# Other query tiles for the side projections of attention, the last gate projection in the last head, and two copies ahead of the token factor

## The chip, the core and the metric

The kernel runs on one core of a Trainium2 chip. A core has TensorE (matrix products into PSUM), VectorE, ScalarE (activations by table), GpSimd, and SyncE, whose queue issues the transfers here. The metric is the device time of one execution in microseconds; lower is better.

## The reference

Two blocks of a network for 1024 tokens of width 1024, in float32:

```
x = x + short_conv_fourier_mixer(rms_norm(x), ...)     # layer 0
x = x + gqa_axial_mixer(rms_norm(x), ...)              # layer 1
x = rms_norm(x)
# second block: pooling and a bidirectional mLSTM, output projection, norm
```

The change lies in layers 0 and 1. Layer 1 is attention with 8 query heads of 128 and 2 key heads:

```
q, k, v, z = split(h @ w_in)
q = rope(rms_norm(q, q_gain));  k = rope(rms_norm(k, k_gain))
p = softmax(q k^T * 128**-0.5)
return ((p v) * silu(z)) @ w_out
```

## The kernel before, in words

Activations lie transposed: channels on partitions, the 1024 tokens along the row. A matrix product with a weight is cut into units of 128 output channels. To keep float32 accuracy, each operand is split into a high and a low part of the type fp32r, and three products are summed (high by high, high by low, low by high). GpSimd splits each weight unit: a cast makes `w_hi` (L600), a subtraction `w_lo` (L602). It has two slots, so unit u can be split when unit u-2 is done; the transfer of the next units runs in three slots of `w_raw`. A unit is 8 blocks of the contraction by 3 products by 2 halves of the tokens, 48 products of 512 columns into one of two PSUM banks, `pair[0]` and `pair[1]`; the engine that reads a bank out signals `pair_free`.

**Layer 0.** The factor of the RMS norm depends on the token alone, so the products run on data that are not normalised, and the factor `rstd_a` is multiplied in afterwards. TensorE makes units 0 and 1 interleaved while the input arrives, then sums the squares (`norm_stats`, L665). ScalarE makes the factor by logarithm and exponential (`norm_rstd`, L1071 and L1072; `ln_ahead`, L1069, is a logarithm of one column that loads the table early) and copies units 0 and 1 out of the banks (`bu`, L1101, and `ax_sb`, L1107). Unit 2 uses the bank of unit 0.

**Layer 1.** For each head h two units are needed: the query projection and the projection of its gate z. They are made during the attention of the head before, by `piece(h, which, c, part)`: `which` is 0 for the query and 1 for z, c is the half of the tokens, and part is one half of the contraction, 12 products at L782. All of them use one half bank, the "side bank", which VectorE or ScalarE must have read out (`bg_free`) before the next use. A head has 8 query tiles of 128 queries, t = 8h + i. For a tile, TensorE makes the scores (L810) two tiles ahead; VectorE takes the maxima (L1631); ScalarE makes the exponentials (L1191); VectorE divides by the sum (L1637, L1638); TensorE transposes the probabilities (`turn`, L823); ScalarE copies the high part (`turned`, L1199) and VectorE subtracts to get the low part (`turned_low`, L1402); and for every pair of tiles TensorE multiplies with the values (`weigh_values`, L835) and VectorE gates the result (L1656).

The next head's query goes a way of its own between these steps: the token factor (`q_token_half`, VectorE, L1605), its square and the swap of its halves (`raw`, ScalarE, L1136 to L1138), the rotation (`q_rotate_half`, VectorE, L1559 and L1562), the sum of its squares (`q_stats`, TensorE, L794), a copy of the sums (`q_sums`, ScalarE, L1172), logarithm and power (`head_ln`, `head_rstd`, L1146 and L1143), scaling (L1567), high and low part (L1150, L1402). The gate takes the token factor (`z_token_half`, L1617) and a Silu (L1185), for which ScalarE loads another table. Every engine works its instructions off in the order in which the code issues them; the order beside the tiles is written out by hand, on TensorE in the table `BESIDE`, on the others by conditions on i. In the last head, ScalarE and VectorE also prepare the operand of the output projection (`y_hi`, L1086, and `low`), from the gated values that went through DRAM.

Of the kernel before, what the change touches and what calls it, by code (L numbers as in the profile page):

```python
# [20 lines left out]
S = 1024  # L21
# [65 lines left out]
def build(nc, x_t, weight_units, channel_params, ident_in, dft_d, dft_s, rope, edge, masks, block_mask,  # L87
          qkv_blocks, gate_w, gate_b, pool_w, reset_mask, out):
    ctx = ExitStack()
    with ctx:  # L90
# [544 lines left out]
        def _(pe):  # L635
# [205 lines left out]
            for c in range(2):  # L841
# [11 lines left out]
            BESIDE = {0: [(0, 0, 0)], 1: [(0, 0, 1)], 2: [(0, 1, 0)], 3: [(0, 1, 1)],  # L853
                      5: [(1, 0, 0), (1, 0, 1)], 6: [(1, 1, 0)], 7: [(1, 1, 1)]}
            for t in range(QT * HEADS):
                h, i = t // QT, t % QT
                turn(t)
                if h + 1 < HEADS and i == 4:
                    q_stats(h + 1, 0)
                if t + 2 < QT * HEADS:  # L860
                    scores(t + 2)
                if h + 1 < HEADS:
                    if i == 4:
                        q_stats(h + 1, 1)
# [183 lines left out]
        def _(act):  # L1048
# [17 lines left out]

            def norm_rstd(count, sums, rstd, bias=eps_col):

                link(act.activation(ln_ahead[:, :], bias[:, :], ACT.Ln, bias=bias[:, :]))  # L1069
# [25 lines left out]
            norm_rstd(1, aux[:, 0:S], rstd_a)  # L1095
            for j in range(AB):
# [11 lines left out]
                signal(pair_free[(u + 1) % 2])  # L1108
                act.wait_ge(fft1_done, j + 1)
# [11 lines left out]
            for e in range(KT):  # L1121
                act.wait_ge(x_done, e + 1)
                gained(e, xa, "norm_odd", opb_hi)
                square(1, e, xa, sq_a, acc_a)
            norm_rstd(2, aux[:, 0:S], rstd_a)


# [3 lines left out]
            def raw(n, c, cols):  # L1131


                act.wait_ge(q_scaled, c + 1)
                half = P // 2
                link(act.activation(sq_b[:, cols], q_raw[:, 0, cols], ACT.Square), qsq)  # L1136
# [16 lines left out]
            for g in range(KV_HEADS):  # L1153
                raw(g, g, whole)
# [11 lines left out]
            def q_raw_half(h, c):  # L1166
                raw(KV_HEADS + h, KV_HEADS + 2 * h + c, columns(c))

            def q_sums(h, c):
# [4 lines left out]
                if c == 1:  # L1174
                    head_ln(rstd_b[:, :], whole)
                    head_rstd()
# [26 lines left out]
            for c in range(2):  # L1203
                q_raw_half(0, c)
# [24 lines left out]
            norm_squares(2, xc, sq_c, acc_c, KT)  # L1229


            norm_rstd(3, aux[:, S:2 * S], rstd_g, eps2_col)
            act.wait_ge(unit_done, BASE[4])
            split_norm(0, op_hi)

            norm_rstd(4, aux[:, 0:S], rstd_c)
# [155 lines left out]
            norm_squares(3, xf, sq_f, acc_f, 2 * KT)  # L1392
            norm_rstd(5, aux[:, 0:S], rstd_f)
# [3 lines left out]
        def _(dve):  # L1397
# [274 lines left out]
            for t in range(QT * HEADS):  # L1672
                h, i = t // QT, t % QT
                beside = h + 1 < HEADS
                if beside and i == 5:
                    scale_head(KV_HEADS + h + 1)
                turned_low(t)
# [14 lines left out]
                if not beside and i >= 1:  # L1692
                    low(i - 1, q_raw[:, (i - 1) % 2, :], OP0["y2"], opb_hi, opb_lo)
            gate_values(4 * HEADS - 1)

            low(KT - 1, y_b[:, (KT - 1) % 2, :], OP0["y2"], opb_hi, opb_lo)
# [397 lines left out]
```

## Time and profile before

| | |
|---|---|
| median of 3 runs | 1993.68 us (1992.86 to 2003.64) |
| the profiled execution | 1993.3 us, its span 1991.5 us |
| TensorE busy | 1819.2 us, 91% |
| VectorE busy | 1047.7 us, 53% |
| ScalarE busy | 582.2 us, 29% |
| GpSimd busy | 427.4 us, 21% |
| mean granted clock of TensorE | 0.968 |

The span is the time from the first to the last instruction of the profiled execution. Busy shares are sums over the whole program; where an engine stands, and for whom, is read from the rows of a stretch. In the timeline a row gives the start, the duration, the engine, the line and operation, the output and inputs, the count of instructions merged into it, and in brackets the idle time of the engine before it with the instruction that ended it. Durations of neighbouring matrix products overlap, so the time that one costs is the difference of two starts. Attention's tiles run from 504.54 to 964.70 us.

### The profile page before, as it was taken

How to read it: one execution, taken by the hardware profiler on the slowest of the kernel's cores; microseconds unless marked ns; L12 is line 12 of the kernel's file. 1: busy time of each engine (PE TensorE's matmuls, PEld its weight loads, DVE VectorE, ACT ScalarE, POOL GpSimd, SP SyncE). 2: the span in 40 equal slices, each digit the busy share in tenths (PEclk: the TensorE clock that was granted, in tenths of full speed). 3: DMA queues.
4: the chain of work that ended last, by engine and by line, in shares of the span. 5: the costliest groups of instructions: out<-in, count | busy, mean ns of one | idle time of the engine just before them, and what ended most of it. 6: DMA issues, size and time to landing. Idle time of an engine off the chain costs nothing. (4 is left out here: it accounts for less than half of the span.)

```text
span 1991.5 us, 21292 instructions
## 1 busy us (share of the span) xinstructions
PE 1819.2 (91%) x8440; PEld 1457.3 (73%) x8440; DVE 1047.7 (53%) x1441; ACT 582.2 (29%) x709; POOL 427.4 (21%) x234
## 2 busy tenths in 40 slices
PE   6999998999899999997896999999998888659996
PEld 5888887877778777776784766777886676447884
DVE  5243244344667676766535653233433788987113
ACT  5010012134555655655103211100225334132001
POOL 3233232232111011010122323333323000003230
PEclk9999999999999999999898999999999999879998
DMA  5011131141000000102420201121231001225102
GB/s 190 32 64 64 43 127 34 52 148 43 12 32 33 32 22 11 33 32 67 172 85 32 74 32 32 69 69 65 91 123 53 22 6 59 85 102 195 53 32 85
DMA packets 36915, 129.75 MB, mean 65 GB/s; under 512 B 4964, under 2 KB 5476, under 8 KB 36560
## 3 DMA queue, kind: packets, MB, share of 16 engines
q1 hardware_dynamic: 36816, 128.39, 18.2%
q8 instruction: 67, 1.10, 0.2%
q14 instruction: 32, 0.26, 0.0%
HBM read 96.68 MB, written 31.56 MB: 64 GB/s over the span
## 5 line engine op out<-in xcount | busy, mean ns | idle before, releaser
L600 POOL CAST w_hi<-w_raw 128x1024 fp32r<-128x1024 f32 x107 | 115.3, 1078 | 1324.9 <-issue 1309.4
L655 PE MATMUL pair<-op_hi,w_hi 128*128 128x512 f32 x1024 | 326.3, 400 | 34.2 <-DVE op_lo L1423 11.7
L655 PE MATMUL pair<-op_lo,w_hi 128*128 128x512 f32 x1024 | 319.1, 393 | 0.0
L655 PE MATMUL pair<-op_hi,w_lo 128*128 128x512 f32 x1024 | 318.6, 392 | 0.0
L602 POOL TENSOR_TENSOR w_lo<-w_raw,w_hi 128x1024 fp32r<-128x1024 f32 x107 | 279.7, 2614 | 8.6
L655 PEld LDWEIGHTS pair<-op_hi,w_hi 128*128 128x128 f32 x1024 | 193.3, 191 | 87.8 <-issue 38.7
L655 PEld LDWEIGHTS pair<-op_lo,w_hi 128*128 128x128 f32 x1024 | 194.8, 190 | 41.3
L655 PEld LDWEIGHTS pair<-op_hi,w_lo 128*128 128x128 f32 x1024 | 194.3, 190 | 41.3
L1402 DVE TENSOR_TENSOR pt_lo<-pair,pt_hi 128x1024 fp32r<-128x1024 f32 x64 | 78.3, 1224 | 106.7 <-ACT pt_hi L1199 106.1
L1199 ACT ACTIVATE pt_hi<-pair 128x1024 fp32r<-128x1024 f32 x64 | 65.7, 1027 | 147.6 <-PE pair L823 91.9
L782 PE MATMUL pair<-opb_hi,w_hi 128*128 128x512 f32 x256 | 100.3, 392 | 0.0
L782 PE MATMUL pair<-opb_hi,w_lo 128*128 128x512 f32 x256 | 99.8, 390 | 0.0
L782 PE MATMUL pair<-opb_lo,w_hi 128*128 128x512 f32 x256 | 99.6, 389 | 0.0
L823 PE MATMUL pair<-ident,prob 128*128 128x128 f32 x512 | 70.1, 282 | 26.6 <-DVE prob L1638 26.6
L823 PEld LDWEIGHTS pair<-ident,prob 128*128 128x128 f32 x512 | 59.2, 144 | 39.2 <-DVE prob L1638 37.3
L655 PE MATMUL pair<-o_hi,w_hi 128*128 128x512 f32 x256 | 80.6, 396 | 6.3 <-DVE o_lo L1402 5.6
L835 PE MATMUL pair<-pt_hi,v_hi 128*128 128x256 f32 x256 | 76.0, 297 | 8.2 <-DVE pt_lo L1402 8.2
L655 PE MATMUL pair<-o_lo,w_hi 128*128 128x512 f32 x256 | 79.8, 393 | 0.0
L655 PE MATMUL pair<-o_hi,w_lo 128*128 128x512 f32 x256 | 79.7, 393 | 0.0
L1631 DVE TENSOR_REDUCE stat_b<-aux 128x1 f32<-128x1024 f32 x64 | 78.4, 1225 | 2.4 <-PE aux L810 0.2
L1014 PE MATMUL aux<-v_tok,k_w 128*128 128x257 f32 x224 | 61.0, 396 | 16.1 <-DVE state L1863 12.9
L835 PE MATMUL pair<-pt_lo,v_hi 128*128 128x256 f32 x256 | 74.9, 292 | 0.0
(294 smaller groups left out, 3072.6 us busy)
## 6 DMA issues: line engine op xcount, KB each, us to landing
w_raw<-weight_units SPq DMA_DIRECT2D x107, 512.0 KB, 3.4
xf<-y_dram SPq DMA_DIRECT2D x14, 512.0 KB, 5.3
xa<-x_t SPq DMA_DIRECT2D x8, 512.0 KB, 8.4
x_dram<-xa SPq DMA_DIRECT2D x8, 512.0 KB, 6.4
xc<-x_dram SPq DMA_DIRECT2D x8, 512.0 KB, 8.2
x_dram<-xc SPq DMA_DIRECT2D x8, 512.0 KB, 2.6
y_dram<-y_d SPq DMA_DIRECT2D x8, 512.0 KB, 2.9
mz_dram<-y_d SPq DMA_DIRECT2D x8, 512.0 KB, 2.9
```

Of the source, the lines that this page charges most:

```text
L600: pool.tensor_copy(w_hi[:, u % 2, :], w_raw[:, u % 3, :]).then_inc(w_hi_done, 1)
L602: pool.tensor_tensor(w_lo[:, u % 2, :], w_raw[:, u % 3, :], w_hi[:, u % 2, :], ALU.subtract).then_inc(w_split, 1)
L655: mm = pe.matmul(acc[:, cols], w, x[:, kt0 + k, cols], start=(first and k == 0 and n == 0), stop=(last and k == KT - 1 and n == 2))
L782: mm = pe.matmul(bank, w, x[:, k, cols], start=(k == 0 and n == 0), stop=(k == KT - 1 and n == 2))
L823: mm = pe.transpose(pair[0][:, k * P:(k + 1) * P], prob[:, t % 2, k * P:(k + 1) * P], ident[:, :])
L835: mm = pe.matmul(pair[1][:, HALF:HALF + 2 * P], v[:, g, k, :], p[:, k, :], start=(k == 0 and n == 0), stop=(k == QT - 1 and n == 2))
L1014: mm = pe.matmul(o, k_w[:, d, i * P:(i + 1) * P], v_tok[:, h % 2, c, :], start=True, stop=True)
L1199: link(act.activation(pt_hi[:, :, (t % 2) * P:(t % 2 + 1) * P], pair[0][:, :].rearrange("p (k q) -> p k q", k=QT), ACT.Copy), pt_hi_ready)
L1402: link(dve.tensor_tensor(lo, full, hi, ALU.subtract), done)
L1631: link(dve.reduce_max(stat_b[:, t % 2, 2:3], aux[:, (t % 2) * S:(t % 2 + 1) * S], AX.X))
```

## The change

In layer 0 the table load for the logarithm is split off (`norm_ahead`), and in the first round ScalarE copies units 0 and 1 out before it makes the factor. The other norms keep the order that they had.

In attention, on TensorE: both parts of a query half stand in tiles 0 and 2, one each before in tiles 0 to 3; the first sum of squares moves from tile 4 to behind the scores of tile 3, the second from behind the scores of tile 4 to ahead of its transposition; the gate's four parts stand one each in tiles 4 to 7, before two in tile 5 and one each in 6 and 7. The gate projection of the last head moves from the head before into tiles 0 and 1 of the last head itself. On VectorE the token factors of the projections move ahead of the tile's subtraction, and the scaling of the head behind it. On ScalarE the square of the second half moves ahead of the copy of tile 3, the swap stays behind. The operand copies of the last head move one tile later.

```diff
-            BESIDE = {0: [(0, 0, 0)], 1: [(0, 0, 1)], 2: [(0, 1, 0)], 3: [(0, 1, 1)],
-                      5: [(1, 0, 0), (1, 0, 1)], 6: [(1, 1, 0)], 7: [(1, 1, 1)]}
+            def beside(t):
+                h, i = t // QT, t % QT
+                if h == HEADS - 1:
+                    for part in range(2):
+                        if i < 2:
+                            piece(h, 1, i, part)
+                    return
+                if i in (0, 2):
+                    for part in range(2):
+                        piece(h + 1, 0, i // 2, part)
+                if i == 3:
+                    q_stats(h + 1, 0)
+                if i >= 4 and h + 1 < HEADS - 1:
+                    piece(h + 1, 1, (i - 4) // 2, i % 2)
+
             for t in range(QT * HEADS):
                 h, i = t // QT, t % QT
+                if i == 4 and h + 1 < HEADS:
+                    q_stats(h + 1, 1)
                 turn(t)
-                if h + 1 < HEADS and i == 4:
-                    q_stats(h + 1, 0)
                 if t + 2 < QT * HEADS:
                     scores(t + 2)
-                if h + 1 < HEADS:
-                    if i == 4:
-                        q_stats(h + 1, 1)
-                    for which, c, part in BESIDE.get(i, []):
-                        piece(h + 1, which, c, part)
+                beside(t)
                 if i % 2:
                     weigh_values(t // 2)
...
-            norm_rstd(1, aux[:, 0:S], rstd_a)
+            norm_ahead()
             for j in range(AB):
...
                 signal(pair_free[(u + 1) % 2])
+                if j == 0:
+                    norm_rstd(1, aux[:, 0:S], rstd_a)
...
                 beside = h + 1 < HEADS
+                if beside and i == 3:
+                    q_square_half(h + 1, 1)
+                if beside and i == 4:
+                    q_sums(h + 1, 1)
                 turned(t)
-                if beside and i == 4:
-                    q_sums(h + 1, 0)
                 if t + 1 < QT * HEADS:
                     exponentials(t + 1)
-                if i == 1:
+                if i == (1 if beside else 2):
                     gate_silu(h)
+                if beside and i == 1:
+                    q_square_half(h + 1, 0)
+                    q_swap_half(h + 1, 0)
+                if beside and i == 3:
+                    q_sums(h + 1, 0)
+                    q_swap_half(h + 1, 1)
                 if beside and i == 4:
-                    q_sums(h + 1, 1)
+                    head_ln(rstd_b[:, :], whole)
+                    head_rstd()
                 if beside and i == 5:
                     q_hi_head(h + 1)
-                if beside and i in (1, 3):
-                    q_raw_half(h + 1, i // 2)
-                if not beside and i >= 1:
-                    y_hi("y2", i - 1, q_raw[:, (i - 1) % 2, :], opb_hi)
+                if not beside and i >= 2:
+                    y_hi("y2", i - 2, q_raw[:, (i - 2) % 2, :], opb_hi)
...
                 beside = h + 1 < HEADS
+                if beside and i in (1, 3):
+                    q_token_half(h + 1, i // 2)
+                if beside and h + 1 < HEADS - 1 and i == 6:
+                    z_token_half(h + 1, 0)
+                if beside and h >= 1 and i == 0:
+                    z_token_half(h, 1)
+                if not beside and i in (1, 2):
+                    z_token_half(h, i - 1)
+                turned_low(t)
                 if beside and i == 5:
                     scale_head(KV_HEADS + h + 1)
-                turned_low(t)
...
-                if beside and i in (1, 3):
-                    q_token_half(h + 1, i // 2)
-                if beside and i in (5, 7):
-                    z_token_half(h + 1, i // 2 - 2)
```

The order on ScalarE at the start of layer 0, before (`bu` and `ax_sb` are the copies of units 0 and 1):

```order
L1069 ACTIVATE ln_ahead<-eps_col 128x1
L1071 ACTIVATE rstd_a<-aux,eps_col 128x1024
L1072 ACT_TABLE_LOAD
L1072 ACTIVATE rstd_a<-rstd_a 128x1024
L1101 ACTIVATE bu<-pair 128x1024
L1107 ACTIVATE ax_sb<-pair 128x1024
```

and now:

```order
L1079 ACTIVATE ln_ahead<-eps_col 128x1
L1114 ACTIVATE bu<-pair 128x1024
L1120 ACTIVATE ax_sb<-pair 128x1024
L1084 ACTIVATE rstd_a<-aux,eps_col 128x1024
L1085 ACT_TABLE_LOAD
L1085 ACTIVATE rstd_a<-rstd_a 128x1024
```

Both copies stand ahead of the factor. The order on VectorE from the gating of tile 2 through tile 3 of a head (`q_raw<-pair,rstd_a` is the token factor of the next query's second half, the two rows of rotation before it belong to the first half), before:

```order
L1656 TENSOR_TENSOR y_b<-pair,sz_q 128x256
L1559 SCALAR_TENSOR_TENSOR q_raw<-q_raw,par,rope_sb 128x512 x2
L1562 TENSOR_TENSOR q_raw<-q_raw 128x512
L1402 TENSOR_TENSOR pt_lo<-pair,pt_hi 128x8x128
L1637 RECIPROCAL stat_b<-stat_b 128x1
L1638 TENSOR_SCALAR prob<-prob,stat_b 128x1024
L1631 TENSOR_REDUCE stat_b<-aux 128x1
L1632 TENSOR_SCALAR stat_b<-stat_b 128x1
L1605 TENSOR_TENSOR q_raw<-pair,rstd_a 128x512
```

and now:

```order
L1689 TENSOR_TENSOR y_b<-pair,sz_q 128x256
L1592 SCALAR_TENSOR_TENSOR q_raw<-q_raw,par,rope_sb 128x512 x2
L1595 TENSOR_TENSOR q_raw<-q_raw 128x512
L1638 TENSOR_TENSOR q_raw<-pair,rstd_a 128x512
L1435 TENSOR_TENSOR pt_lo<-pair,pt_hi 128x8x128
L1670 RECIPROCAL stat_b<-stat_b 128x1
L1671 TENSOR_SCALAR prob<-prob,stat_b 128x1024
L1664 TENSOR_REDUCE stat_b<-aux 128x1
L1665 TENSOR_SCALAR stat_b<-stat_b 128x1
```

The token factor moved from the end of tile 3 to ahead of its subtraction, directly behind the rotation. The order on ScalarE from tile 3 on (`sq_b<-q_raw` is the square, `sq_b<-pair` the copy of the sums, `q_raw<-q_raw` the swap), before:

```order
L1199 ACTIVATE pt_hi<-pair 128x8x128
L1191 ACTIVATE prob,stat_b<-aux,stat_b 128x1024
L1136 ACTIVATE sq_b<-q_raw 128x512
L1137 ACTIVATE q_raw<-q_raw 64x512
L1138 ACTIVATE q_raw<-q_raw 64x512
L1199 ACTIVATE pt_hi<-pair 128x8x128
L1172 ACTIVATE sq_b<-pair 128x512
L1191 ACTIVATE prob,stat_b<-aux,stat_b 128x1024
L1172 ACTIVATE sq_b<-pair 128x512
```

and now:

```order
L1150 ACTIVATE sq_b<-q_raw 128x512
L1218 ACTIVATE pt_hi<-pair 128x8x128
L1210 ACTIVATE prob,stat_b<-aux,stat_b 128x1024
L1194 ACTIVATE sq_b<-pair 128x512
L1155 ACTIVATE q_raw<-q_raw 64x512
L1156 ACTIVATE q_raw<-q_raw 64x512
L1194 ACTIVATE sq_b<-pair 128x512
L1218 ACTIVATE pt_hi<-pair 128x8x128
L1210 ACTIVATE prob,stat_b<-aux,stat_b 128x1024
```

The square stands ahead of the copy of tile 3, and both copies of the sums ahead of the copy of tile 4.

## Rows read from the trace of the kernel before

**Rows 1.** Busy time by stretch: window, us, busy (instructions) of each engine, clock, DMA.

```profile
35.90:42.60 6.70, 1.88 (x5) 0.59 (x4) 0.05 (x1) 4.54 (x5) 3.38 (x2) 0.94 0.47 157
42.60:67.31 24.71, 24.71 (x97) 20.15 (x98) 15.99 (x20) 0.95 (x1) 3.44 (x2) 0.88 0.06 22
504.54:851.30 346.76, 326.16 (x1849) 276.12 (x1850) 239.47 (x335) 193.76 (x240) 42.22 (x24) 1.00 0.07 24
851.30:910.26 58.96, 55.57 (x311) 47.05 (x310) 39.99 (x56) 32.29 (x40) 7.19 (x5) 0.97 0.08 28
910.26:964.70 54.44, 36.14 (x198) 31.32 (x197) 35.17 (x46) 27.66 (x32) 0.91 (x1) 0.81 0.45 164
```

**Rows 2.** Timeline of TensorE around the first sum of squares.

```profile
35.90 1.88 PE L665 MATMUL aux<-acc_a,ones 128*128 128x512 f32 x4
...
42.60 0.76 PE L655 MATMUL pair<-op_hi,w_hi 128*128 128x512 f32 x1 [4.83 <-ACTq L81]
```

**Rows 3.** Timeline of TensorE in the second head: tiles 1, 2, 4 and 5.

```profile
567.34 1.04 PE L823 MATMUL pair<-ident,prob 128*128 128x128 f32 x8
...
569.59 0.39 PE L782 MATMUL pair<-opb_hi,w_hi 128*128 128x512 f32 x1
...
572.31 0.28 PE L835 MATMUL pair<-pt_hi,v_hi 128*128 128x256 f32 x1
...
575.18 1.03 PE L823 MATMUL pair<-ident,prob 128*128 128x128 f32 x8
...
589.34 1.04 PE L823 MATMUL pair<-ident,prob 128*128 128x128 f32 x8
...
594.06 1.10 PE L794 MATMUL pair<-sq_b,ones 128*128 128x512 f32 x2 [1.37 <-ACTq L81]
596.36 1.09 PE L823 MATMUL pair<-ident,prob 128*128 128x128 f32 x8 [1.21 <-DVE prob L1638]
```

**Rows 4.** Timeline of ScalarE in the second head: tiles 1 and 4.

```profile
568.46 1.02 ACT L1199 ACTIVATE pt_hi<-pair 128x1024 fp32r<-128x1024 f32 x1 [2.75 <-issue]
569.52 1.12 ACT L1191 ACTIVATE prob<-aux,stat_b 128x1024 f32<-128x1024 f32 x1
...
574.05 0.63 ACT L1136 ACTIVATE sq_b<-q_raw 128x512 f32<-128x512 f32 x1 [0.95 <-DVE q_raw L1605]
...
595.98 1.28 ACT L1146 ACT_TABLE_LOAD   x1
...
599.73 1.06 ACT L1143 ACTIVATE sq_b<-sq_b 128x1024 f32<-128x1024 f32 x1
```

**Rows 5.** Timeline of VectorE in the second head: tiles 1 and 2.

```profile
569.52 1.22 DVE L1402 TENSOR_TENSOR pt_lo<-pair,pt_hi 128x1024 fp32r<-128x1024 f32 x1 [0.84 <-ACT pt_hi L1199]
...
582.79 1.54 DVE L1559 SCALAR_TENSOR_TENSOR q_raw<-q_raw,par,rope_sb 128x512 f32<-128x512 f32 x2
584.37 0.69 DVE L1562 TENSOR_TENSOR q_raw<-q_raw 128x512 f32<-128x512 f32 x1
```

**Rows 6.** Timeline of GpSimd at three weight units.

```profile
138.88 2.35 POOL L602 TENSOR_TENSOR w_lo<-w_raw,w_hi 128x1024 fp32r<-128x1024 f32 x1
...
443.41 1.04 POOL L600 CAST w_hi<-w_raw 128x1024 fp32r<-128x1024 f32 x1 [9.14 <-issue]
444.53 3.21 POOL L602 TENSOR_TENSOR w_lo<-w_raw,w_hi 128x1024 fp32r<-128x1024 f32 x1
...
586.24 1.04 POOL L600 CAST w_hi<-w_raw 128x1024 fp32r<-128x1024 f32 x1 [22.98 <-issue]
```

**Rows 7.** Timeline of VectorE beside the first two of these.

```profile
139.12 3.20 DVE L1467 TENSOR_TENSOR u_pad<-u_pad,rstd_a 128x1024 f32<-128x1024 f32 x1
...
443.53 2.00 DVE L1562 TENSOR_TENSOR q_raw<-q_raw 128x1024 f32<-128x1024 f32 x1
```

**Rows 8.** Timeline of TensorE in tiles 3 and 4 of the last head.

```profile
932.13 0.39 PE L835 MATMUL pair<-pt_hi,v_hi 128*128 128x256 f32 x1 [1.94 <-DVE pt_lo L1402]
...
936.60 1.03 PE L823 MATMUL pair<-ident,prob 128*128 128x128 f32 x8
```

More of the change, by code:

```diff
@@ L1065, in gained, with norm_ahead @@
                 link(act.activation(hi[:, k, :], x[:, k, :], ACT.Copy, scale=col(gain, k)), hi_ready)
+            def norm_ahead(bias=eps_col):
+                link(act.activation(ln_ahead[:, :], bias[:, :], ACT.Ln, bias=bias[:, :]))
             def norm_rstd(count, sums, rstd, bias=eps_col):
[L1069 removed]
                 act.wait_ge(stat_done, count)
@@ L1124, in _ @@
                 square(1, e, xa, sq_a, acc_a)
+            norm_ahead()
             norm_rstd(2, aux[:, 0:S], rstd_a)
@@ L1129, in _, with raw_square, raw_swap @@
             act.wait_ge(x_stored, 16 * KT)
-            def raw(n, c, cols):
+            def raw_square(c, cols):
                 act.wait_ge(q_scaled, c + 1)
+                link(act.activation(sq_b[:, cols], q_raw[:, 0, cols], ACT.Square), qsq)
+            def raw_swap(cols):
                 half = P // 2
-                link(act.activation(sq_b[:, cols], q_raw[:, 0, cols], ACT.Square), qsq)
                 link(act.activation(q_raw[0:half, 1, cols], q_raw[half:P, 0, cols], ACT.Copy))
@@ L1153, in _ @@
             for g in range(KV_HEADS):
-                raw(g, g, whole)
+                raw_square(g, whole)
+                raw_swap(whole)
                 act.wait_ge(qstat, g + 1)
@@ L1164, in columns, with q_square_half, q_swap_half @@
                 return slice(c * HALF, (c + 1) * HALF)
-            def q_raw_half(h, c):
-                raw(KV_HEADS + h, KV_HEADS + 2 * h + c, columns(c))
+            def q_square_half(h, c):
+                raw_square(KV_HEADS + 2 * h + c, columns(c))
+            def q_swap_half(h, c):
+                raw_swap(columns(c))
             def q_sums(h, c):
@@ L1173, in q_sums @@
                 signal(bg_free)
-                if c == 1:
-                    head_ln(rstd_b[:, :], whole)
-                    head_rstd()
             def q_hi_head(h):
@@ L1203, in _ @@
             for c in range(2):
-                q_raw_half(0, c)
+                q_square_half(0, c)
+                q_swap_half(0, c)
             for c in range(2):
                 q_sums(0, c)
+            head_ln(rstd_b[:, :], whole)
+            head_rstd()
             q_hi_head(0)
@@ L1211, in _ @@
                 beside = h + 1 < HEADS
+                if beside and i == 3:
+                    q_square_half(h + 1, 1)
+                if beside and i == 4:
+                    q_sums(h + 1, 1)
                 turned(t)
-                if beside and i == 4:
-                    q_sums(h + 1, 0)
                 if t + 1 < QT * HEADS:
                     exponentials(t + 1)
-                if i == 1:
+                if i == (1 if beside else 2):
                     gate_silu(h)
+                if beside and i == 1:
[4 more added lines that the diff above has]
+                    q_swap_half(h + 1, 1)
                 if beside and i == 4:
-                    q_sums(h + 1, 1)
+                    head_ln(rstd_b[:, :], whole)
+                    head_rstd()
                 if beside and i == 5:
                     q_hi_head(h + 1)
-                if beside and i in (1, 3):
-                    q_raw_half(h + 1, i // 2)
-                if not beside and i >= 1:
-                    y_hi("y2", i - 1, q_raw[:, (i - 1) % 2, :], opb_hi)
+                if not beside and i >= 2:
+                    y_hi("y2", i - 2, q_raw[:, (i - 2) % 2, :], opb_hi)
+            y_hi("y2", KT - 2, q_raw[:, (KT - 2) % 2, :], opb_hi)
             y_hi("y2", KT - 1, y_b[:, (KT - 1) % 2, :], opb_hi)
             norm_squares(2, xc, sq_c, acc_c, KT)
+            norm_ahead(eps2_col)
             norm_rstd(3, aux[:, S:2 * S], rstd_g, eps2_col)
@@ L1234, in _ @@
             split_norm(0, op_hi)
+            norm_ahead()
             norm_rstd(4, aux[:, 0:S], rstd_c)
@@ L1392, in _ @@
             norm_squares(3, xf, sq_f, acc_f, 2 * KT)
+            norm_ahead()
             norm_rstd(5, aux[:, 0:S], rstd_f)
@@ L1687, in _ @@
                     q_lo_head(h + 1)
-                if beside and i in (1, 3):
-                    q_token_half(h + 1, i // 2)
-                if beside and i in (5, 7):
-                    z_token_half(h + 1, i // 2 - 2)
-                if not beside and i >= 1:
-                    low(i - 1, q_raw[:, (i - 1) % 2, :], OP0["y2"], opb_hi, opb_lo)
+                if not beside and i >= 2:
+                    low(i - 2, q_raw[:, (i - 2) % 2, :], OP0["y2"], opb_hi, opb_lo)
             gate_values(4 * HEADS - 1)
+            low(KT - 2, q_raw[:, (KT - 2) % 2, :], OP0["y2"], opb_hi, opb_lo)
             low(KT - 1, y_b[:, (KT - 1) % 2, :], OP0["y2"], opb_hi, opb_lo)
```

## Prediction

> **What bounds the kernel now.** I read the page's busy shares first: TensorE is busy for 91% of the span, VectorE for 53%, ScalarE for 29%, so time is lost only where TensorE stands. The sums by stretch [rows 1] then show where the change acts: the 24.71 us of the first two whole units behind the token factor, six heads of attention in 346.76 us (57.79 each), the seventh in 58.96 and the last in 54.44, where TensorE is busy for 36.14 us only and the granted clock is 0.81. Last I read the timeline of one regular head, the second, on four engines [rows 3 to 7]; the reader is to see what TensorE waits for inside a head and what stands in the queues of ScalarE and VectorE in front of what it waits for.
>
> **The start.** TensorE issues the sums of squares at 35.90, needs 1.88 us, and then stands 4.83 us until ScalarE has made the token factor and copied unit 0 out [rows 2]. The copies now come first; unit 1 ends at 35.9 and unit 0 three blocks of six products, some 4 us, sooner, so unit 0's bank is free before the sums end, and unit 2 can start at 37.8: 4.8 us sooner. Units 2 and 3 are 96 matrix products of 512 columns. Twelve of them take 569.59 to 572.31 = 2.72 us at full clock [rows 3], so 96 take 21.8, against 24.71 [rows 1]: 2.9 us go to the clock, granted at 0.88 behind the idle stretch. With no idle stretch ahead that goes too. Sum: -7.8 us. What the factor feeds (VectorE's folding) is needed only behind unit 3, 21.8 us later, and the factor itself comes no later than before, so that stays hidden; if it did not, the Fourier step would wait by as much. The later uses of the factor keep their order and cost nothing.
>
> **A tile of attention.** From rows 3 to 5, with T for the start of a tile's transposition: transposition and scores 569.59 - 567.34 = 2.25 us of TensorE, one part of a projection (12 products) 2.72, the weighing of values behind each odd tile 575.18 - 572.31 = 2.87, and one sum of squares about 0.9 of its 1.10 [rows 3]. ScalarE copies the transposed tile from T+1.12 to 2.15 and makes the next exponential until 3.4; VectorE's subtraction ends at T+3.4 [rows 4, 5], so the weighing of an odd tile cannot start before T+3.46, and the next transposition (factor and scaling, 0.95 us behind the exponential) not before T+4.5.
>
> **What is moved in a head.** TensorE's work stays the same, 53.2 us a head: 8 x 2.25 + 8 x 2.72 + 4 x 2.87 + 2 x 0.9 = 53.1. What changes is cover. Before, a part stood in each of tiles 0 to 3, and the largest waits were 1.37 us before the second sum of squares and 1.21 behind it [rows 3]. Now two parts stand in tiles 0 and 2, none in 1 and 3. The walk through a head:
> - Tile 0: 2.25 + 2 x 2.72 = 7.7. Nothing waits.
> - Tile 1: no part, so the weighing waits for 3.46 instead of 2.25: 3.46 + 2.87 = 6.35.
> - Tile 2: 7.7 on TensorE. ScalarE's Silu, square and swaps of tile 1 end 0.5 us later relative to this tile, since the 0.95 us wait ahead of the square [rows 4] goes but tile 1 is 7.84 - 6.35 = 1.5 shorter. VectorE's rotation, before at 582.79, 7.61 behind the transposition of 575.18 [rows 3, 5], then starts at T+8.1.
> - Tile 3: this is the step on which most hangs. VectorE has the second half's token scaling now ahead of its subtraction, but behind the rotation, and ScalarE has the square of that half ahead of the copy that the tile's weighing needs. Even with a free path the rotation (1.54 + 0.69) ends at 10.35 behind tile 2's start, the scaling at 11.0, the square at 11.7, the copy at 12.8, the subtraction at 14.1; before, the copy waited for nothing but the transposition. And the path is not free. The last part of the query projection now ends at T+7.7 of tile 2, which lets GpSimd split the next unit: before, at 586.24, behind the rotation [rows 6]; now cast at 8.0, subtraction from about 9.1. While GpSimd is in its subtraction, VectorE's operation on two SBUF operands does not advance: 139.12 took 3.20 us instead of 1.22, to 1.1 behind GpSimd's end, and at 443.53 one stood behind the cast (2.00), after which GpSimd took 3.21 instead of 2.35 [rows 6, 7]. The rotation's three operations are all of that kind. Walking them against the cast (to 8.9) and the subtraction (9.5 to 11.9): the first ends at 9.65, the second starts at 11.75, the third ends at 13.2. Scaling 14.0, square 14.7, copy 15.75, subtraction 17.0, weighing 17.05 to 19.9, second sum of squares 0.9: tile 4 starts 20.85 behind tile 2. Before it was 589.34 - 575.18 = 14.2 [rows 3], with half the parts in these two tiles.
> - Tile 4: 2.25 + 2.72 = 5.0. ScalarE's logarithm and power (595.98 to 600.79) [rows 4] end at T+8.3.
> - Tile 5: its copy waits for them, so the subtraction ends 5.6 behind the tile's start and the weighing waits 0.65: 8.5.
> - Tile 6: the next head's scores wait for the query's low part, 1.3: 6.25. Tile 7: 2.25 + 2.72 + 2.87 = 7.85.
>
> Sum 7.7 + 6.35 + 20.85 + 5.0 + 8.5 + 6.25 + 7.85 = 62.5 us, against 57.5 in the second head. (The window of six heads [rows 1] has its mean at 57.79.) The clock comes on top. In tile 3 TensorE stands some 4.0 and 2.1 us around one sum of squares. In the last head of before it stood 1.94 us ahead of a weighing that then took 936.60 - 932.13 = 4.47 instead of 2.87 us [rows 8], so 1.6 us each. I take 1.5 us a head; nothing at one end, the 2.9 of the start at the other. Six heads: 6 x (64.0 - 57.79) = +37.2 us.
>
> **The path shared with GpSimd.** The rows decide by themselves; the Trainium skill ("SBUF — State Buffer", section "SBUF: two separate sides") calls the shared ports an exclusive lock, held for the whole instruction, against VectorE operations with two SBUF inputs. By that rule the rotation stands as in my walk and a head takes 62.5 us; without it 59.6. The trace agrees with the lock: 3.20 against 1.22 [rows 5, 7].
>
> **The seventh head** has no gate parts now: same to tile 4 (34.9), then 4.5, then 9.0 (the copy of tile 5 waits for the power), 4.5 and 3.46 + 2.87: 59.2, and with two falls of the clock 62.2, against 58.96: +3.2.
>
> **The last head** takes the four parts into tiles 0 and 1: 7.7 and 2.25 + 5.44 + 2.87 = 10.6. Tile 2 takes 4.5; Silu and its table now stand there, with a table load again before tile 3's exponential, and a copy of the output operand is between: 7.8 for tile 3. Then 11.8, 4.5 and 7.1 to the next unit: 54.0 at full clock. At full clock the same walk of before is 4.5 + 6.35 for tiles 0 and 1, some 13.4 for the next two, then 11.8 and 11.6, together 47.7; what lies between that and 54.44 [rows 1], 6.7 us, is the clock (0.81). Tiles 0 and 1 thus grow by 18.3 - 10.85 = 7.4 for 10.9 us of work. The clock falls behind tile 1 as before, 6.3 of the 6.7: 60.3, +6.0. The operand copies moved one tile later cost nothing: ScalarE and VectorE stand idle while the last values are weighed (2.87 us or more), and the last two fit in; without that cover they cost 1.2 us once.
>
> **Sum.** -7.8 + 37.2 + 3.2 + 6.0 = +38.6. The profiled execution took 1993.3 us (span 1991.5), the median is 1993.68: 2032 us.
>
> **The rivals.**
> - The lock does not bite: the cast comes late enough, or the rotation slips through. Tile 4 then starts 17.95 behind tile 2, a head is 59.6 + 1.5. Six heads +20, seventh 0, last +6, start -7.8: 2012. For it speaks that cast and rotation are 0.1 us apart in my walk; against it that either order puts the subtraction into the rotation.
> - Faster: the queues don't stand in tile 3. If the rotation ends before tile 3 is transposed, the weighing waits for T+3.46 only; the two waits around the sums of squares (1.37, 1.21) are gone and a head is 53.1 + 1.2 + 0.3 + 0.7 + 1.3 = 56.6. Six heads -7, seventh -6, last +6, start -7.8: 1979. It decides from the point where the rotation ends under T+7.7 of tile 2; the row has it at 9.88 behind tile 2's start already before, so it needs ScalarE to be over 2 us ahead of my walk.
> - No change: the tile 3 wait is there but small (half of that without the lock, no clock loss), and pays off the start: 1993 plus or minus 9.
>
> **Chances.** Main 0.56, with its own range 2021 to 2043 (no clock loss at one end, 2.9 a head at the other, less a more favourable order at the lock). Without the lock 0.19, no change 0.11, faster 0.14. The range 2003 to 2043 leaves the faster case and most of no change out. About 0.5% (10 us) is what a measurement tells from no change: faster 0.14, same 0.10, slower 0.76.
>
> **What would show it.** Unit 2 starting at 37.8 and ending by 49. In a regular head: a wait of about 1.2 us at the weighing of tile 1, about 6 us of standing in tile 3, VectorE's rotation operations at 2 us or more instead of 0.77, heads of 62 to 65 us. Wrong would be: heads under 58, rotation operations of unchanged length, or a last head under 54 us.

## The result, and the profile after

The changed kernel takes 2035.01 us (median of 4 runs, 2034.21 to 2043.51) against 1995.35 us (1992.86 to 2003.64, 4 runs) for the kernel before: ratio 1.0201, 95% interval 1.0160 to 1.0242. It is slower. Forecast were 2032 us and a range of 2003 to 2043.

The profiled execution is the slowest of the four, 2043.51 us (span 2041.7, mean clock 0.954; the other three runs have 0.959 to 0.960). The page's line of busy time:

```profile
PE 1841.3 (90%) x8440; PEld 1474.4 (72%) x8440; DVE 1067.2 (52%) x1441; ACT 582.4 (29%) x709; POOL 428.1 (21%) x234
```

TensorE is busy for 22 us more than before with the same products, which says that some of them ran at a lower clock. Where the time lies is seen in the sums by stretch, the same as in [rows 1] (window, us, then PE, PEld, DVE, ACT, POOL, the granted clock, DMA); the last row is tile 3 of the second head with its two waits:

```profile
39.22:62.74 23.52, 23.52 (x101) 18.77 (x100) 15.96 (x20) 4.49 (x4) 6.88 (x4) 1.00 0.20 67
499.76:891.35 391.59, 344.21 (x1849) 290.28 (x1850) 253.26 (x335) 193.78 (x240) 41.93 (x24) 0.93 0.06 21
891.35:956.02 64.67, 48.70 (x263) 41.22 (x261) 40.90 (x54) 32.30 (x40) 4.63 (x3) 0.89 0.07 25
956.02:1014.18 58.16, 45.50 (x247) 39.32 (x245) 35.34 (x47) 27.67 (x32) 3.42 (x2) 0.85 0.30 106
588.73:604.16 15.43, 10.71 (x44) 8.04 (x42) 9.46 (x10) 4.71 (x7) 3.72 (x2) 0.67 0.00 1
```

From the first sum of squares to the end of unit 3 it is 23.52 us, where it was 67.31 - 35.90 = 31.41. The six regular heads take 391.59 us instead of 346.76, the seventh 64.67 instead of 58.96, the last 58.16 instead of 54.44. TensorE at the start, where a row of [rows 2] had 4.83 us of waiting:

```profile
39.22 1.88 PE L665 MATMUL aux<-acc_a,ones 128*128 128x512 f32 x4
40.53 1.04 PE L655 MATMUL pair<-op_hi,w_hi 128*128 128x512 f32 x2
```

Unit 2 now follows the sums without a gap. The sums themselves come 3.3 us later than in the execution of before, though the order ahead of them is the same. GpSimd could start its second cast only at 7.96 us, when the transfer of the weights had landed, instead of 7.00. Its work then stood beside an operation of VectorE that makes the low part of the input:

```profile
13.97 3.27 DVE L1456 SCALAR_TENSOR_TENSOR op_lo<-xa,par,op_hi 128x1024 fp32r<-128x1024 f32 x1
17.29 1.22 PE L655 MATMUL pair<-op_hi,w_hi 128*128 128x512 f32 x2 [3.02 <-DVE op_lo L1456]
16.00:20.00 4.00, 2.71 (x6) 2.15 (x7) 3.90 (x4) 2.91 (x4) 0.15 (x1) 0.54 1.05 409
```

That operation took 3.27 us instead of 1.28, TensorE waited 3.02 us for it, where it had waited 1.53 at that point before, and from 16 to 20 us the granted clock was 0.54 instead of 1.00.

In attention, the reader should look at the second head, at tiles 2 and 3. The table gives the time of each tile in us, from the start of its transposition to the start of the next one on TensorE's timeline, with tiles 2 and 3 as one sum:

```
tile          0     1     2+3    4     5     6     7     head
before      5.01  7.84  14.16  7.02 10.64  5.01  7.84   57.52
forecast    7.7   6.35  20.85  5.0   8.5   6.25  7.85   62.5 + 1.5 for the clock
after       7.73  6.44  23.17  4.99  8.60  6.20  7.83   64.96
```

TensorE in tile 3 of that head:

```profile
588.73 1.03 PE L823 MATMUL pair<-ident,prob 128*128 128x128 f32 x8
...
595.01 2.05 PE L794 MATMUL pair<-sq_b,ones 128*128 128x512 f32 x2 [3.88 <-DVEq L81]
597.90 0.58 PE L835 MATMUL pair<-pt_hi,v_hi 128*128 128x256 f32 x1 [0.84 <-DVE pt_lo L1435]
598.28 0.42 PE L835 MATMUL pair<-pt_lo,v_hi 128*128 128x256 f32 x1
...
603.19 1.13 PE L794 MATMUL pair<-sq_b,ones 128*128 128x512 f32 x2
604.16 0.60 PE L823 MATMUL pair<-ident,prob 128*128 128x128 f32 x4
```

It stands 3.88 us ahead of the first sum of squares and 0.84 us behind it. The forecast had some 4.0 and 2.1; the second wait is shorter because the sum of squares itself took 2.05 us where it had been 1.10 [rows 3]. The weighing (24 products of 256 columns) then needs 603.19 - 597.90 = 5.29 us, where it was 2.87 [rows 3]: its products start 0.21 us apart instead of 0.12, at the lower of the clock's two levels (1.2 GHz) throughout. In the sums of tile 3 the granted clock is 0.67. What the first wait was for stands in VectorE's rows, with GpSimd's and ScalarE's beside them:

```profile
589.01 4.35 DVE L1592 SCALAR_TENSOR_TENSOR q_raw<-q_raw,par,rope_sb 128x512 f32<-128x512 f32 x2
593.39 0.69 DVE L1595 TENSOR_TENSOR q_raw<-q_raw 128x512 f32<-128x512 f32 x1
594.12 0.69 DVE L1638 TENSOR_TENSOR q_raw<-pair,rstd_a 128x512 f32<-128x512 f32 x1
596.62 1.23 DVE L1435 TENSOR_TENSOR pt_lo<-pair,pt_hi 128x1024 fp32r<-128x1024 f32 x1 [1.81 <-ACT pt_hi L1218]
```

```profile
589.01 1.04 POOL L600 CAST w_hi<-w_raw 128x1024 fp32r<-128x1024 f32 x1 [21.28 <-issue]
590.13 2.68 POOL L602 TENSOR_TENSOR w_lo<-w_raw,w_hi 128x1024 fp32r<-128x1024 f32 x1
```

```profile
594.90 0.63 ACT L1150 ACTIVATE sq_b<-q_raw 128x512 f32<-128x512 f32 x1 [8.89 <-DVE q_raw L1638]
595.57 1.02 ACT L1218 ACTIVATE pt_hi<-pair 128x1024 fp32r<-128x1024 f32 x1
```

The first two operations of the rotation take 4.35 us instead of 1.54 [rows 5]: 1.59 us for the one that starts together with GpSimd's cast, 2.73 for the other, 0.75 each before. The second ends 0.55 us behind GpSimd's subtraction (592.81). Only then come, in this order, the rotation's third operation, the token scaling of the second half, ScalarE's square, the copy of the transposed tile, which TensorE had finished at 588.73 + 1.03 = 589.76, and the subtraction that the weighing waits for.

### The profile page after: what moved, and what is told of

Its sections match the earlier page's. It is cut to its first block and busy times, and to the rows that moved or that the text cites. A ratio compares the mean times of both kernels' runs of the same rounds, so it can differ in the third digit from the quotient of the medians.

```text
span 2041.7 us, 21285 instructions
## 1 busy us (share of the span) xinstructions
PE 1841.3 (90%) x8440; PEld 1474.4 (72%) x8440; DVE 1067.2 (52%) x1441; ACT 582.4 (29%) x709; POOL 428.1 (21%) x234
## 5 line engine op out<-in xcount | busy, mean ns | idle before, releaser
L835 PE MATMUL pair<-pt_hi,v_hi 128*128 128x256 f32 x256 | 85.7, 335 | 30.4 <-DVE pt_lo L1435 30.4
L835 PEld LDWEIGHTS pair<-pt_hi,v_hi 128*128 128x128 f32 x256 | 59.2, 231 | 45.7 <-DVE pt_lo L1435 45.4
L835 PE MATMUL pair<-pt_lo,v_hi 128*128 128x256 f32 x256 | 82.5, 322 | 0.0
L835 PE MATMUL pair<-pt_hi,v_lo 128*128 128x256 f32 x256 | 82.2, 321 | 0.0
```

What stands on the lines that cost most here:

```text
L835: mm = pe.matmul(pair[1][:, HALF:HALF + 2 * P], v[:, g, k, :], p[:, k, :], start=(k == 0 and n == 0), stop=(k == QT - 1 and n == 2))
```

## The experiments

**The start by itself.** Before, with the copies of units 0 and 1 ahead of the token factor:

```diff
-            norm_rstd(1, aux[:, 0:S], rstd_a)
+            norm_ahead()
             for j in range(AB):
...
                 signal(pair_free[(u + 1) % 2])
+                if j == 0:
+                    norm_rstd(1, aux[:, 0:S], rstd_a)
                 act.wait_ge(fft1_done, j + 1)
```

> The kernel before with the change of the start alone: the first two units are copied out ahead of the token factor, attention is untouched. Theory (the start is worth what its terms say): unit 2 starts as soon as the sums of squares end, units 2 and 3 take about 22 us, attention starts some 7.8 us sooner, and the whole kernel is 7.8 us faster than before, with the rest unchanged. Rival A: only the idle stretch goes and the clock stays as it was behind it: 4.8 us. Rival B: what the start gives is taken back by a later stage that waits for something else (a transfer, VectorE's folding): 0 to 2 us.

Measured: 1987.3 us (1985.99 to 1991.78), ratio to before 0.9945 [0.9927, 0.9964], so 7 to 15 us faster. The first row is the start, the others are the six heads, the seventh and the last:

```profile
37.35:60.85 23.50, 23.50 (x101) 18.77 (x100) 15.95 (x20) 4.49 (x4) 6.85 (x4) 1.00 0.21 67
495.66:846.80 351.14, 330.52 (x1848) 279.74 (x1849) 239.49 (x335) 193.75 (x240) 42.21 (x24) 0.98 0.07 23
846.80:907.15 60.35, 56.95 (x311) 48.08 (x310) 39.99 (x56) 32.28 (x40) 7.20 (x5) 0.94 0.08 27
907.15:959.54 52.39, 34.12 (x199) 29.66 (x197) 35.17 (x46) 27.67 (x32) 0.91 (x1) 0.87 0.46 170
```

The stretch is 23.50 us against 31.41: 7.9 us, and the clock in it is 1.00 where it was 0.88 behind the wait [rows 1]. Unit 2 starts 5.4 us sooner behind the sums, and units 2 and 3 take 22.2 us instead of 24.71. Both halves of the term are there, and rivals A (4.8 us) and B (0 to 2 us) fall. The rows of attention tell something else: its code is that of before, and it still takes 351.14 us instead of 346.76. The last section comes back to that.

**Attention by itself.** The changed kernel, with the token factor ahead of the copies again:

```diff
             norm_ahead()
+            norm_rstd(1, aux[:, 0:S], rstd_a)
             for j in range(AB):
...
-                if j == 0:
-                    norm_rstd(1, aux[:, 0:S], rstd_a)
```

> The changed kernel with the start of before (the token factor ahead of the copies of units 0 and 1): the change of attention alone. Theory (the terms add up): 7.8 us slower than the changed kernel and so about 46 to 48 us slower than before. Rival: the start's gain is already lost in the changed kernel, and this one takes the same time as it.

Measured: 2045.22 us (2042.64 to 2047.30), ratio to before 1.0228 [1.0201, 1.0256], 40 to 51 us slower. Its median lies 10.2 us above that of the changed kernel, but the two were taken beside different runs of before (1999.67 and 1995.35); by the ratios the distance is 5 us. The heads are the same to 0.2 us (64.90 in the second). The start, from the sums to the end of unit 3, takes 66.68 - 36.51 = 30.17 us here against 23.52, so the gain is there in the changed kernel, and all that is lost is lost in attention. The stretch is 1.2 us shorter than in the execution of before (31.41), with the same wait of 4.83 us in it: the clock's half of the start's gain differs from one execution to the next, 2.5 us by one and 1.3 by the other.

**GpSimd's split later.** Nothing in the order of VectorE or ScalarE is changed; GpSimd starts on the next query unit only when the second half of the query is scaled:

```diff
                 pool.wait_ge(w_loaded[u % 3], 16 * (u // 3 + 1))
+                if BASE[2] + 8 <= u <= BASE[3] and u % 2 == BASE[2] % 2:
+                    pool.wait_ge(q_scaled, KV_HEADS + 2 * ((u - BASE[2] - 4) // 2))
```

> The changed kernel, but GpSimd splits the next unit's weights in attention (cast and subtraction) only once VectorE has scaled the second half of the next head's query, so that it can't run beside the rotation. VectorE's and ScalarE's order is unchanged. Theory (VectorE's rotation does not advance while GpSimd works): the rotation's first two operations take about 1.54 us for the two instead of 4.35, it ends at about 10.3 behind tile 2's start instead of 13.1, the weighing of tile 3 and all behind it come 2.9 us sooner, six heads and the seventh together 20 us less; up to 33 us less if the low clock behind the shorter wait shrinks too. Rival (the queue order alone makes the wait, GpSimd's work costs nothing): the rotation stays slow or nothing behind it moves, 0 us.

Measured: 2007.41 us (2006.24 to 2010.28), ratio to before 1.0045 [1.0028, 1.0061]; against the changed kernel's 1.0201 that is 31 us less, near the upper end of what was expected (20 to 33). In its second head VectorE and GpSimd have:

```profile
578.63 1.54 DVE L1594 SCALAR_TENSOR_TENSOR q_raw<-q_raw,par,rope_sb 128x512 f32<-128x512 f32 x2
580.21 0.69 DVE L1597 TENSOR_TENSOR q_raw<-q_raw 128x512 f32<-128x512 f32 x1
```

```profile
581.74 1.04 POOL L602 CAST w_hi<-w_raw 128x1024 fp32r<-128x1024 f32 x1 [24.39 <-DVE q_raw L1640]
582.86 2.36 POOL L604 TENSOR_TENSOR w_lo<-w_raw,w_hi 128x1024 fp32r<-128x1024 f32 x1
```

and TensorE in tile 3, which starts at 578.35:

```profile
581.83 1.10 PE L796 MATMUL pair<-sq_b,ones 128*128 128x512 f32 x2 [1.07 <-DVEq L81]
584.71 0.39 PE L837 MATMUL pair<-pt_hi,v_hi 128*128 128x256 f32 x1 [1.79 <-DVE pt_lo L1437]
```

The rotation has its length of before again, 2.81 us less, and the wait ahead of the sum of squares is 1.07 us instead of 3.88, 2.81 less. So GpSimd's work made the rotation long, and the rotation's end set the wait, one for one. That is 7 x 2.81 = 19.7 us. Most of the rest lies where the clock fell less: tile 3 is 3.7 us shorter and not 2.8, the first head's tile 0 is 1.6 us shorter and the seventh's tile 5 1.2. Tiles 2 and 3 take 7.73 + 11.7 = 19.4 us in five of the six heads, with a low clock in the weighing (granted 0.85 in tile 3), and 7.73 + 10.19 = 17.92 in the fourth, without one (1.00). The forecast's walk without the shared path had 17.95. The rival (0 us) falls.

**The rotation later.** The changed kernel, with the first half's rotation at the end of tile 3; GpSimd's split is where the change put it:

```diff
-                if beside and i in (2, 4):
-                    q_rotate_half(h + 1, i // 2 - 1)
+                if beside and i in (3, 4):
+                    q_rotate_half(h + 1, i - 3)
```

> The changed kernel, but VectorE does the first half's rotation at the end of tile 3 instead of the end of tile 2, so it stands neither in front of the token scaling of the second half nor of the subtraction of tile 3. The split on GpSimd stays where it was. Theory (the wait in tile 3 is the rotation in front of the scaling, the square and the copy): the weighing of tile 3 starts at about 12 behind tile 2's start instead of 17.9, tile 4 at 15.8 instead of 23.2, a head takes 57.5 to 58.5 us, and the whole kernel about 1985 to 1992 us, some 45 us less than the changed kernel. Rival A (the scaling and the square ahead of the copy make the wait, whatever the rotation does): less than 10 us of gain. Rival B: the rotation is late for the second half now, so the next head's scores in tile 6 wait instead, and half of the gain is lost: 2008 to 2015 us.

Measured: 1985.49 us (1982.85 to 1989.73), ratio to before 0.9935 [0.9911, 0.9959]; by the ratios some 53 us less than the changed kernel, by the medians 49.5; 45 were expected. All of the loss is gone. Six heads, the seventh, the last, and tile 3 of the second head:

```profile
494.56:839.60 345.04, 324.84 (x1849) 275.06 (x1850) 236.40 (x335) 193.90 (x240) 40.16 (x24) 1.00 0.07 24
839.60:897.21 57.61, 46.48 (x262) 39.34 (x261) 38.10 (x54) 32.32 (x40) 4.34 (x3) 0.94 0.08 28
897.21:955.45 58.24, 44.62 (x246) 38.73 (x245) 35.34 (x47) 27.68 (x32) 3.42 (x2) 0.88 0.31 107
574.26:582.16 7.90, 7.10 (x43) 5.50 (x42) 5.79 (x9) 4.72 (x7) 3.41 (x2) 1.00 0.00 1
```

Tile 3 takes 7.90 us instead of 15.43, at clock 1.00. A regular head takes 57.45 us (the first 57.79), where 57.5 to 58.5 were expected, and in tile 6 nothing new is late (6.21 us as in the changed kernel). Rivals A and B fall. VectorE and GpSimd in tile 3:

```profile
574.54 0.69 DVE L1638 TENSOR_TENSOR q_raw<-pair,rstd_a 128x512 f32<-128x512 f32 x1
577.04 1.23 DVE L1435 TENSOR_TENSOR pt_lo<-pair,pt_hi 128x1024 fp32r<-128x1024 f32 x1 [1.82 <-ACT pt_hi L1218]
```

```profile
574.54 1.04 POOL L600 CAST w_hi<-w_raw 128x1024 fp32r<-128x1024 f32 x1 [21.27 <-issue]
575.66 2.38 POOL L602 TENSOR_TENSOR w_lo<-w_raw,w_hi 128x1024 fp32r<-128x1024 f32 x1
```

The token scaling stands beside GpSimd's cast and the tile's subtraction beside GpSimd's, and both keep their lengths (0.69 and 1.23 us): one input of each is in PSUM. The rotation, with all its inputs in SBUF, took 4.35 us instead of 1.54 beside the same work of GpSimd in the changed kernel. The section of the Trainium skill that the forecast weighed ("SBUF — State Buffer", "SBUF: two separate sides") names VectorE operations with two SBUF inputs, and besides them those in a two-port performance mode; for the two-input ones the trace agrees on both sides of that line. An operation with one tensor from SBUF was slowed too, the scaling of the probabilities in the kernel before, beside the cast at 586.24 [rows 6]:

```profile
586.55 1.28 DVE L1638 TENSOR_SCALAR prob<-prob,stat_b 128x1024 f32<-128x1024 f32 x1
```

It takes 0.75 us elsewhere. The rows don't say in which mode it ran.

**Products in the waits.** The changed kernel, with products that nobody reads in the two waits of tile 3, into a bank that is free there:

```diff
+            def fill(t, n):
+
+                pe.wait_ge(yq_done, t // 2)
+                for _ in range(n):
+                    pe.matmul(pair[1][:, HALF:HALF + 2 * P], k_hi[:, 0, 0:P], k_hi[:, 0, 0:2 * P],
+                              start=True, stop=True)
...
                 if i == 3:
+                    fill(t, 32)
                     q_stats(h + 1, 0)
+                    fill(t, 14)
```

> The changed kernel, and TensorE makes products whose result is never used (32 and 14 products of 256 columns, some 3.6 and 1.6 us at full clock) in the two waits of tile 3, ahead of the first sum of squares and behind it. Nothing else moves. Theory (the low clock of the weighing in tile 3 comes from the two waits ahead of it): the granted clock stays high there, the weighing takes 2.9 us instead of 5.3, tiles 2 and 3 take 20.9 us instead of 23.1, the kernel is 7 times 2.2 = 15 us faster than the changed kernel. Rival A: the clock falls anyway, since what counts is not that TensorE stands there: no gain. Rival B: the products in vain are longer than the waits and push the weighing back: slower by up to 7 us.

Measured: 2022.2 us (2020.47 to 2023.01), ratio to before 1.0127 [1.0097, 1.0156]; by the ratios 15 us less than the changed kernel, as expected, and 12.8 by the medians, with 46 products more in each head. TensorE in tile 3 of the second head, and the sum of that tile:

```profile
585.36 3.99 PE L857 MATMUL pair<-k_hi 128*128 128x256 f32 x32
589.44 1.10 PE L794 MATMUL pair<-sq_b,ones 128*128 128x512 f32 x2
589.97 2.23 PE L857 MATMUL pair<-k_hi 128*128 128x256 f32 x14
592.33 0.38 PE L835 MATMUL pair<-pt_hi,v_hi 128*128 128x256 f32 x1
```

```profile
583.11:596.15 13.04, 12.82 (x89) 11.20 (x88) 9.51 (x10) 4.72 (x7) 3.76 (x2) 1.00 0.01 2
```

The clock is 1.00 where it was 0.67, the weighing takes 595.29 - 592.33 = 2.96 us instead of 5.29, and tiles 2 and 3 take 20.77 us, where the walk without any clock loss had 20.85. Five of the six regular heads are 62.60 us (walk: 62.5), the first 64.52. VectorE's rotation still takes 4.39 us, so nothing but the clock was taken away. Rivals A and B fall: the waits ahead of the weighing had cost it the clock.

**The last head's gate projection by itself.** Before, with that one part of the change:

```diff
                     for which, c, part in BESIDE.get(i, []):
-                        piece(h + 1, which, c, part)
+                        if which == 0 or h + 1 < HEADS - 1:
+                            piece(h + 1, which, c, part)
+                elif i < 2:
+                    for part in range(2):
+                        piece(h, 1, i, part)
```

with the token scalings of that gate in the last head, and its Silu and the operand copies one tile later to match.

> The kernel before with one part of the change: the gate projection of the last head (four parts, 48 products) is made in tiles 0 and 1 of the last head instead of beside the seventh, with its Silu and the copies of the output operand one tile later. Start, regular heads and the sums of squares are as before. Theory (the terms of the forecast, corrected by the changed kernel's trace): the seventh head becomes 0 to 3 us shorter, the last head 3.7 to 6 us longer, together +2 to +5 us; a term that can't be told from no change in the time, but can in the two stretches of the trace. Rival: the parts fill time that the last head wastes (TensorE was busy for 36 of its 54 us), the two heads together get 5 us shorter or more.

Measured: 2006.33 us (1995.54 to 2011.07, 12 runs), ratio to before 1.0043 [1.0023, 1.0063]. The stretches:

```profile
502.90:863.17 360.27, 339.66 (x1848) 286.85 (x1849) 239.51 (x335) 193.78 (x240) 42.16 (x24) 0.95 0.07 23
863.17:921.24 58.07, 48.59 (x262) 40.67 (x261) 38.61 (x54) 32.28 (x40) 4.67 (x3) 0.88 0.08 28
921.24:979.47 58.23, 45.48 (x247) 39.32 (x245) 35.35 (x47) 27.68 (x32) 3.42 (x2) 0.85 0.30 106
```

The seventh is 0.9 us shorter and the last 3.8 longer. Together they take 116.30 us against 113.40 before [rows 1] and 112.74 in the kernel with the start alone: +2.9 to +3.6, in the expected range, and the rival (5 us shorter) falls. The time as a whole rises by 5 to 13 us, and most of that the edit can't have caused: the six regular heads, whose code is that of before, take 360.27 us instead of 346.76 in this execution. 12 us of the difference are in tile 5, which takes 12.2 to 13.5 us here, and before 10.64 in five heads and 12.01 in one; the rest is in the first head's tile 0 (6.64 instead of 5.05). So the ratio does not measure the edit; the two stretches do.

**The parts put together.** The kernel with the later rotation, and the last head's gate projection back beside the seventh:

```diff
                 if h == HEADS - 1:
-                    for part in range(2):
-                        if i < 2:
-                            piece(h, 1, i, part)
                     return
...
-                if i >= 4 and h + 1 < HEADS - 1:
+                if i >= 4:
                     piece(h + 1, 1, (i - 4) // 2, i % 2)
```

with the Silu, the token scalings and the operand copies of the last head one tile earlier to match.

> The parts put together that were worth something: the start of the changed kernel, its attention with the first half's rotation at the end of tile 3, but the last head's gate projection beside the seventh head, as before. Theory (the terms add up): the seventh and the last head together take 110 to 113 us instead of the 115.9 us of the kernel with the later rotation alone, so 3 to 5 us less than that one's 1985.5: 1981 to 1983 us, which is 0.7 to 0.9% less than the kernel before. Rival: the seventh head, with gate parts again, falls to the low clock at its fifth tile and the last head at its third, and nothing is gained: 1985 us or more.

Measured: 1979.99 us (1976.55 to 1984.91), ratio to before 0.9915 [0.9888, 0.9943]: 11 to 22 us faster than before, in the range expected (0.7 to 0.9%), and the lowest median of all that ran. Its interval overlaps that of the kernel with the later rotation (0.9911 to 0.9959), so that it is faster than that one is likely, not shown by the times. Seventh and last head:

```profile
843.97:901.41 57.44, 54.12 (x311) 45.84 (x309) 39.48 (x56) 32.30 (x40) 6.83 (x5) 1.00 0.08 28
901.41:953.95 52.54, 34.88 (x199) 30.02 (x197) 35.19 (x46) 27.67 (x32) 0.91 (x1) 0.84 0.47 170
```

Together 109.98 us instead of 57.61 + 58.24 = 115.85. The expected gain was 3 to 5 us, and it is 5.9, since the seventh head with its four gate parts (48 products) is no longer than without them: with the parts TensorE had work while it waited, and the clock stays at 1.00; without them tile 5 took 11.43 us instead of 8.63. The rival falls. Not all of the 5.9 us is seen in attention as a whole, which is 3.1 us shorter in this execution: the first head's tile 0 took 10.63 us here, at a granted clock of 0.72, where it took 7.77 at 1.00 with the same order of work.

## Why the forecast was right, and where it was off

The mechanism was that of the forecast. A regular head of attention comes apart into its three causes, each with a kernel that lacks it (the third row is the one head of six in that kernel without a fall of the clock; the other five take 61.2 to 61.6 us):

```
                                                   measured    the forecast's walk
the changed kernel                                  64.9
without the low clock (products in the waits)       62.60      62.5
without GpSimd beside the rotation (and no fall)    59.72      59.6
without the rotation ahead of the scaling           57.45      57.5 (made for that run)
```

- **The start.** Forecast -7.8 us, measured 31.41 - 23.52 = -7.9, and -7.9 in the kernel with the start alone. Both parts, the wait (5.4 us, forecast 4.8) and the clock behind it (2.5, forecast 2.9), were right, and nothing later took it back. The clock's part is that of one execution of before; against the start in the kernel with attention alone it would be 1.3.
- **Tiles 0, 1 and 4 to 7.** Each within 0.1 us of the walk. The waits named there are in the trace: 1.05 us at the weighing of tile 1 (1.2 was forecast).
- **Tile 3.** The rotation ended 13.09 us behind tile 2's start (13.2), VectorE's subtraction 16.86 (17.0). In the walk the cast came 0.1 us ahead of the rotation; in the trace both start together, and the first rotation operation ends at 9.61 (9.65).
- **The clock in tile 3** is the term that was mis-sized: 1.5 us a head against 2.3, since the weighing ran at the low clock from its first product to its last. The first head had a fall in tile 0 as well (9.37 us instead of 7.73, granted 0.82), which no term had. Six heads are +44.8 us instead of +37.2.
- **The seventh head** is +5.7 instead of +3.2, by the same term: 2.2 in tile 3, and 11.43 in tile 5 where the walk had 9.0, with 1.5 for each; tiles 6 and 7 are 0.7 over the walk.
- **The last head** is +3.7 instead of +6.0 (the forecast's own 60.3 - 54.44 gives 5.9). The first four tiles are as in the walk (7.73, 10.56, 4.50, 7.97 against 7.7, 10.6, 4.5, 7.8), and the whole is 4.2 us over the walk's 54.0 instead of the 6.3 taken for the clock. How far that term can be told is limited from the other side: with its gate projection made beside the seventh head the last head took 54.44, 52.39 and 52.54 us in three executions. Against the latter two the move costs 5.6 to 5.8.
- **The sum** of the measured terms is -7.9 + 44.8 + 5.7 + 3.7 = +46.3, with the 3.3 by which the sums of squares come later +49.6, and the profiled execution is 2043.51 - 1993.3 = 50.2 us above that of before. The median is only 41.3 us above the median that stood there (1993.68), near the forecast's 38.6. The other three executions are 8 to 9 us shorter and have a slightly higher clock (0.959 to 0.960 against 0.954); what of that lies at the start and what in attention isn't shown by any row. So the nearness of the median is in part luck: by the profiled executions the forecast's terms were 7.7 us too small in sum (46.3 against 38.6), of which 10.1 lie in the seven heads and -2.3 in the last.

The rivals: without GpSimd beside the rotation the kernel would have been 6 to 12 us slower than before (the run with GpSimd later), where the forecast had 18 (2012). The faster case needed the rotation out of the way, and a kernel with just that is 8 to 18 us faster than before, where the forecast had 15 (1979), with heads of 57.45 us for its 56.6. No change would have needed a small wait in tile 3; it was 4.7 us. What decided against all three is a single place in the head, tile 3, where TensorE and ScalarE both waited for the same operation of VectorE.

## What to carry to other kernels

Before an operation is moved ahead of another in an engine's queue, write down what stands in front of it there at that moment, and what another engine is let go by the same step; here one step ended a projection earlier, which released GpSimd into VectorE's rotation, and another put a chain that TensorE waited for directly behind that rotation. The cure was to move an operation that nobody needed yet behind the one that all needed: one condition, some 50 us. A wait of TensorE can cost more than its length: 4.7 us of waits in tile 3 cost the weighing behind them another 2.3 us.

## What the runs showed of the hardware

The low clock does not follow from the rows alone. In the kernel with only the start changed, the fourth and the fifth head have the same two waits ahead of tile 5's products:

```profile
701.56 1.10 PE L794 MATMUL pair<-sq_b,ones 128*128 128x512 f32 x2 [1.38 <-ACTq L81]
703.86 0.87 PE L823 MATMUL pair<-ident,prob 128*128 128x128 f32 x6 [1.21 <-DVE prob L1647]
...
759.08 1.10 PE L794 MATMUL pair<-sq_b,ones 128*128 128x512 f32 x2 [1.37 <-ACTq L81]
761.38 0.90 PE L823 MATMUL pair<-ident,prob 128*128 128x128 f32 x3 [1.21 <-DVE prob L1647]
```

Behind the first pair tile 5 took 10.64 us, behind the second 13.46. In the same way tile 3 took 10.19 us in one head of the kernel with GpSimd's split later, and 11.7 in the five others, with one order of work. And the first head's tile 0, behind the same wait of 2.7 us each time, took 7.77 us in two executions with the new order, 9.35 to 9.42 in three and 10.63 in one. Attention in the order of before thus gives heads of 57.5 to 60.4 us, from one head and one execution to the next, so that a profiled execution is a sample: a stretch whose code is untouched differed by 13.5 us between two of them (360.27 and 346.76). The runs of the kernel before spread from 1990.95 to 2008.26 us (15 runs on one chip), those with the last gate projection moved from 1995.54 to 2011.07 (12 runs), though those with the start alone, with the same attention, only from 1985.99 to 1991.78 (6 runs). With the sums of squares in their new places tile 5 takes 8.6 us in every regular head of all six executions, that of the changed kernel and those of five experiments, wherever the rotation stands. That these kernels had no fall in tile 5 is thus seen; whether such falls are all of the spread of the others, and how much of the last kernel's gain is their absence, no run here takes apart.
